# Sublayer boundaries of a two-block transformer kernel: TensorE sums x and the scaled branch in its transposes, token tile 0 is finished first, and GpSimd updates x later

## The chip, the cores and the metric

One Trainium2 chip, one of its cores. The metric is the device time of one execution in microseconds (us); less is better. Three runs of the kernel before stand beside it, and one more execution was taken with the profiler. The engines are named as the profile names them: PE (TensorE, with PEld for its weight loads), DVE (VectorE), ACT (ScalarE), POOL (GpSimd) and SP (SyncE, which here only issues the weight loads).

## What is computed

256 tokens of width 1024 pass two transformer blocks. Cut to what the change touches:

```python
def rms_norm_2(x, g):
    xf = x.astype(jnp.float32)
    y = xf * lax.rsqrt(jnp.mean(xf * xf, axis=-1, keepdims=True) + EPS)
    return (y * g.astype(jnp.float32)).astype(x.dtype)

def swiglu(x, w_gate, w_up, w_down):
    return (jax.nn.silu(x @ w_gate) * (x @ w_up)) @ w_down

for layer in range(DEPTH_2):                      # second block, 2 layers
    if layer == N_A_LAYERS:
        k, v, c = shared_kv(h, kv_norm_g, w_kv, w_fgate, b_fgate)
    f = swiglu(rms_norm_2(h, ffn1_pre_g[layer]), ffn1_w_gate[layer], ffn1_w_up[layer], ffn1_w_down[layer])
    h = h + 0.5 * rms_norm_2(f, ffn1_post_g[layer])
    hn = rms_norm_2(h, mix_pre_g[layer])
    m = recurrent_block(hn, ...) or forgetting_attention(hn, ...)
    h = h + rms_norm_2(m, mix_post_g[layer])
    f = swiglu(rms_norm_2(h, ffn2_pre_g[layer]), ...)
    h = h + 0.5 * rms_norm_2(f, ffn2_post_g[layer])
```

The first block has a mixer, then a mixture of 32 experts (`moe`), each added to x without a norm behind it. All arithmetic is float32.

## The kernel before

**Tiling.** The 256 tokens are two tiles of 128 partitions, t = 0 and t = 1. The residual stream is `x_res` (128 x 2 x 1024). A sublayer reads it transposed, with the channels on the partitions: `xT_hi` and `xT_lo` (8 pieces k of 128 channels, 256 tokens). A float32 product is made of three fast ones (`mm3`, L614): hi x hi, hi x lo, lo x hi, where hi is a value rounded to the fast format and lo is what is missing. Weights stream in pieces of 128 x 1024 through a ring of six slots: SP loads `raw`, ACT writes `w_hi` (`hi`, L1236, or in loops L1301), DVE writes `w_lo = raw - w_hi` (`lo`, L1687, or in loops L1698). The semaphores `hi_done`, `lo_done` and `used` count pieces; ACT may write piece i when piece i - 6 is used.

**Order.** Nothing plans at run time: each engine's program is written out by hand, and the engines meet at counting semaphores. An engine that waits holds back all that stands behind it in its own program.

**A feed-forward** (`feed_forward`, L684, L1303, L1771) takes for each of its 22 (or 32) column blocks f three weight pieces: gate and up (24 products of 256 columns each, into PSUM banks 4 to 7) and down (12 or 24 products of 512 columns, accumulated in banks 0 to 3, two banks for each token tile). DVE multiplies the gate by the row factor `rb` (L1752), ACT applies silu (L1296), and DVE makes the hidden block in `hidden` (times up, times `rb`, for the experts times their weight, then the hi and lo halves, L1758 to L1768). PE runs one block ahead: gate and up of f + 1 come before down of f. The last down writes tile 0, increments `y0_done`, then writes tile 1.

**A boundary between two sublayers** is what the change is about. The program calls them by the number n of the norm that follows: n = 1 (mixer to experts) and n = 2 (experts to the first feed-forward) have a plain residual (`residual`, L1811). n = 3 (feed-forward to recurrent block), 4 (back), 5 (feed-forward to keys and values), 7 (feed-forward to attention), 8 (attention to feed-forward) and the end of the kernel have a norm of the branch y first (`post_norm`, L1821). n = 6 reuses x of n = 5. One with a post norm runs, for each tile t:

1. ACT squares y from PSUM with a row sum and takes the root (`y_squares`, L1333). At n = 3, 5, 7 and the end it starts tile 0 at `y0_done`; at n = 4 and 8 it waits for both tiles.
2. DVE makes the row factor in five tiny steps (`row_rsqrt`, L1714), then `xn = y * factor * gain` (L1828) and `x_res = xn + x_res` (L1831). The gain `g_post` has been broadcast by a DMA from POOL's queue (L581).
3. PE waits for `x_ready`, transposes the eight pieces of the tile into PSUM (L645), and keeps itself at work with dummy products before and between (`keep_warm`, L622; the counts are in the table `WARM`).
4. ACT squares `x_res` for the next norm (`statistics`, L1256), and writes `xT_hi` from the transposes with the gain of the norm (`gained`, L1246); DVE writes `xT_lo` (L1735).
5. PE waits until all four groups of `xT_lo` are there (`xT_ready`), then starts the next sublayer. The row factor of the norm is applied later: DVE makes a diagonal matrix of it (`diag`, L1747), PE spreads it over the partitions with `ones` (`spread`, L651), ACT copies it to `rb` (L1288).

In the code that follows, `channel_major` (L677) is the product of one weight piece with all of xT into one bank.

## Time and profile before

| | us |
|---|---|
| median of 3 runs | 1646.89 |
| lowest, highest | 1646.74, 1649.29 |
| the profiled execution, its own time | 1646.3 |
| its span (first to last instruction) | 1644.5 |
| PE busy in it | 1588.8 (97%) |
| DVE busy | 1062.0 (65%) |
| ACT busy | 784.8 (48%) |
| POOL busy | 43.6 (3%) |
| chain that ended last: share of PE, of DVE | 86%, 8% |

All times of instructions count from the span's start. A product on PE overlaps the next, so a row of `x1` with 0.39 us can be followed by one that starts 0.23 us later; the pace is the distance of the starts. A float32 product that is not split (the dummies, the diagonal spread) is two rows of the trace; a transpose is one. Dummy products count as busy: at a boundary PE's busy share says nothing of useful work. That is why the boundaries are read from the timeline of each engine, from the last product of the old sublayer to the first of the new one.

### The profile page before, as it was taken

To read this page: it belongs to the slowest core of one execution; us is meant where nothing else is said; L and a number is where in the kernel's file an instruction comes from. 1 tells how busy PE (TensorE), PEld (TensorE's weight loads), DVE (VectorE), ACT (ScalarE), POOL (GpSimd) and SP (SyncE) were. 2 spreads that over 40 slices of the span, in tenths; PEclk is the share of its full clock that TensorE was granted. 3 is DMA by queue.
4 is the path that set the end of the run, shared out by engine and by line. 5 is a ranking of instruction groups with operands and counts; after the bars stand their busy time and mean duration, and the time that the engine had idled before them with its cause. 6 is when DMAs were issued, how large, how long until landed. Compare 5 with 4: busy or idle time off the path is not lost.

```text
span 1644.5 us, 27400 instructions
## 1 busy us (share of the span) xinstructions
PE 1588.8 (97%) x10220; PEld 1435.5 (87%) x10220; DVE 1062.0 (65%) x1912; ACT 784.8 (48%) x1151; POOL 43.6 (3%) x68
## 2 busy tenths in 40 slices
PE   8999899999999999999999999999999999999997
PEld 6877778899999899998777999988999989889996
DVE  5358654667666686667585766666766666476665
ACT  6464434444444544435775544455544456454442
POOL 2200000000000300000000000000000000000000
PEclk9999999999999999999999999999999999999999
DMA  8841142755555476664433666645666643356661
GB/s 288 213 154 61 42 145 75 294 184 181 178 189 191 136 215 182 180 190 135 128 97 97 191 181 180 190 128 167 197 187 191 191 130 116 90 167 191 186 183 52
DMA packets 258199, 266.13 MB, mean 162 GB/s; under 512 B 9408, under 2 KB 209392, under 8 KB 257760
## 3 DMA queue, kind: packets, MB, share of 16 engines
q1 hardware_dynamic: 254704, 255.87, 50.7%
q0 software_dynamic: 3440, 9.54, 1.9%
q8 instruction: 33, 0.54, 0.1%
q14 instruction: 22, 0.18, 0.0%
HBM read 264.21 MB, written 1.09 MB: 161 GB/s over the span
## 4 chain that ended last, share of the span: by engine, by line
PE 86%; DVE 8%; ACT 2%; issue 2%; DMA 1%; POOL 0%; DVEq 0%; SPq 0%; ACTq 0%
PE ps L616 27%; PE ps L617 26%; PE ps L618 26%; DVE xT_lo L1735 2%; PE ps L1026 2%; DVE w_lo L1693 1%; DMA arena<-comb_dram 1%; DVE xn L1828 1%; PE ps L626 1%; PE ps L1138 1%; DVE arena L1913 0%; ACT sq L1341 0%; DVE small L1912 0%; PE ps L1148 0%; DVE arena L1938 0%
## 5 line engine op out<-in xcount | busy, mean ns | idle before, releaser
L616 PE MATMUL ps<-xT_hi,w_hi 128*128 128x256 f32 x1696 | 482.9, 285 | 5.9 <-DVE w_lo L1698 3.5
L617 PE MATMUL ps<-xT_lo,w_hi 128*128 128x256 f32 x1696 | 480.6, 283 | 0.0
L618 PE MATMUL ps<-xT_hi,w_lo 128*128 128x256 f32 x1696 | 480.6, 283 | 0.0
L1301 ACT ACTIVATE w_hi<-raw 128x1024 fp32r<-128x1024 f32 x300 | 316.3, 1060 | 246.7 <-PE ps L618 241.9
L1698 DVE TENSOR_TENSOR w_lo<-raw,w_hi 128x1024 fp32r<-128x1024 f32 x300 | 357.4, 1219 | 8.9 <-DMA arena<-comb_dram 8.0
L616 PEld LDWEIGHTS ps<-xT_hi,w_hi 128*128 128x128 f32 x1696 | 325.7, 192 | 12.2 <-DVE xT_lo L1735 4.5
L617 PEld LDWEIGHTS ps<-xT_lo,w_hi 128*128 128x128 f32 x1696 | 325.7, 192 | 3.7
L618 PEld LDWEIGHTS ps<-xT_hi,w_lo 128*128 128x128 f32 x1696 | 325.8, 192 | 0.0
L1693 DVE TENSOR_TENSOR w_lo<-raw,w_hi 128x1024 fp32r<-128x1024 f32 (+4 forms) x185 | 217.8, 1211 | 71.8 <-ACT w_hi L1243 66.8
L1243 ACT ACTIVATE w_hi<-raw 128x1024 fp32r<-128x1024 f32 (+4 forms) x185 | 186.8, 1049 | 70.4 <-PE ps L618 70.4
L616 PE MATMUL ps<-w_hi,hid_hi 128*128 128x512 f32 x480 | 188.5, 393 | 4.4 <-DVE hid_lo L1768 3.1
L1296 ACT ACTIVATE hid_sil<-hid_sil 128x256 f32<-128x256 f32 x120 | 50.5, 421 | 290.0 <-DVE hid_sil L1752 290.0
L617 PE MATMUL ps<-w_lo,hid_hi 128*128 128x512 f32 x480 | 188.0, 392 | 0.0
L618 PE MATMUL ps<-w_hi,hid_lo 128*128 128x512 f32 x480 | 186.8, 389 | 0.0
L1752 DVE TENSOR_TENSOR hid_sil<-ps,rb 128x256 f32<-128x256 f32 x120 | 50.9, 424 | 169.8 <-PE ps L618 154.2
L616 PE MATMUL ps<-w_hi,xT_hi 128*128 128x512 f32 (+3 forms) x392 | 151.8, 387 | 3.8 <-DVE w_lo L1693 2.0
L618 PE MATMUL ps<-w_hi,xT_lo 128*128 128x512 f32 (+3 forms) x392 | 149.7, 382 | 0.0
L617 PE MATMUL ps<-w_lo,xT_hi 128*128 128x512 f32 (+3 forms) x392 | 149.5, 381 | 0.0
L1758 DVE TENSOR_TENSOR hid_sil<-hid_sil,ps 128x256 f32<-128x256 f32 x120 | 50.5, 421 | 147.6 <-PE ps L618 146.5
L616 PEld LDWEIGHTS ps<-w_hi,hid_hi 128*128 128x128 f32 x480 | 90.5, 189 | 21.0 <-DVE hid_lo L1768 3.7
L618 PEld LDWEIGHTS ps<-w_hi,hid_lo 128*128 128x128 f32 x480 | 90.1, 188 | 19.6
L617 PEld LDWEIGHTS ps<-w_lo,hid_hi 128*128 128x128 f32 x480 | 90.5, 189 | 14.6
(338 smaller groups left out, 1991.1 us busy)
## 6 DMA issues: line engine op xcount, KB each, us to landing
raw<-in_ffn_w_gate_dram SPq DMA_DIRECT2D x88, 512.0 KB, 4.1
raw<-in_ffn_w_up_dram SPq DMA_DIRECT2D x88, 512.0 KB, 5.3
raw<-in_ffn_w_down_dram SPq DMA_DIRECT2D x88, 512.0 KB, 4.3
raw<-in_w_in_dram SPq DMA_DIRECT2D x40, 512.0 KB, 5.6
raw<-in_w_gate_dram SPq DMA_DIRECT2D x32, 512.0 KB, 3.6
raw<-in_w_up_dram SPq DMA_DIRECT2D x32, 512.0 KB, 4.0
raw<-in_w_down_dram SPq DMA_DIRECT2D x32, 512.0 KB, 3.6
raw<-in_rg_w_in_dram SPq DMA_DIRECT2D x16, 512.0 KB, 4.8
```

Of the source, the lines that this page charges most:

```text
L616: pe.matmul(o, a_hi, b_hi, start=start, stop=False)
L617: pe.matmul(o, a_hi, b_lo, start=False, stop=False)
L618: return pe.matmul(o, a_lo, b_hi, start=False, stop=stop)
L1026: m = pe.matmul(ps[0:c1 - j * RB, 4 + 2 * z + j // 2, (j % 2) * T:(j % 2 + 1) * T], w[:, g, at:at + c1 - j * RB], cv[:, i, :], start=i == ...
L1243: act.activation(w_hi[0:parts, i % RING, 0:cols], raw[0:parts, i % RING, 0:cols], ACT.Copy)\
L1296: act.activation(sil[:, par, :], sil[:, par, :], ACT.Silu).then_inc(silu_done, 1)
L1301: act.activation(w_hi[:, s, :], raw[:, s, :], ACT.Copy).then_inc(hi_done, 1)
L1693: dve.tensor_tensor(w_lo[0:parts, s, 0:cols], raw[0:parts, s, 0:cols], w_hi[0:parts, s, 0:cols].bitcast(F32), ALU.subtract).then_inc(lo_do ...
L1698: dve.tensor_tensor(w_lo[:, s, :], raw[:, s, :], w_hi[:, s, :].bitcast(F32), ALU.subtract)\
L1735: m = dve.scalar_tensor_tensor(XT[n][1][o], ps[:, 4 + j, k * P:(k + 1) * P], gcol[:, n, 4 * g + k:4 * g + k + 1], XT[n][0][o].bitcast(F32) ...
L1752: dve.tensor_tensor(sil[:, par, :], ps[:, 4 + par, 0:T], rb[:], ALU.mult).then_inc(gate_scaled, 1)
L1758: dve.tensor_tensor(hid[:, par, :], sil[:, par, :], ps[:, 6 + par, 0:T], ALU.mult).then_inc(hid_mul, 1)
```

## The change

For the five boundaries with a post norm and a sublayer behind them:

- DVE makes only `xn = y * gain` (in two halves of 512 columns, `y_gained`), without the row factor. ACT squares each half by itself, in the opposite order, so that both read different banks. The row factor goes into `diag` (`y_diag`).
- PE makes for each of the eight pieces of a tile two float32 products into one PSUM region: x times the identity, and xn times `diag`. The sum is the transposed new x. `x_res` itself is updated later by POOL (`tensor_scalar`, then `tensor_tensor`, 128 x 1024 each), after PE has read the tile.
- The squares of x for the next norm (`statistics`) wait for that update, behind `gained` on ACT.
- The last two down steps of a feed-forward are done for tile 0 first, then for tile 1; likewise the last pieces of the recurrent block's and the attention's output products.
- `first_pair` starts the next sublayer with the products that need only `xT_hi`, half by half, in banks 0 and 1, and makes those with `xT_lo` last. The recurrent block starts with token tile 0 alone (`first_chunk`).
- In `hidden` the product with the up half comes last, behind `rb` and the expert weight, and one `lo` is put between.
- The residuals of n = 1 and 2 are made in halves (`x_part`, `x_ready`). The dummy counts are smaller, the output leaves in four transfers.

```diff
@@ pool (j = 1 to 5)
+                    jn = (3, 4, 5, 7, 8)[j - 1]
+                    for t in range(NT):
+                        pool.wait_ge(y_gained, 4 * (j - 1) + 2 * t + 2)
+                        pool.wait_ge(y_rstd, 2 * (j - 1) + t + 1)
+                        pool.wait_ge(norm_tr, 4 * jn + 2 * t + 2)
+                        pool.tensor_scalar(xn[:, t, :], xn[:, t, :], s_(S_YR + t), None, ALU.mult).then_inc(sig("y_scaled"), 1)
+                        pool.wait_ge(sig("y_scaled"), 2 * (j - 1) + t + 1)
+                        pool.tensor_tensor(x_res[:, t, :], xn[:, t, :], x_res[:, t, :], ALU.add).then_inc(x_ready, 1)
@@ pe
-            WARM = {0: (0, 0, 0), 1: (2, 2, 8), 2: (0, 2, 7), 3: (7, 4, 6), 4: (10, 5, 6), 5: (7, 4, 6), 6: (0, 0, 0),
-                    7: (7, 4, 6), 8: (10, 5, 6)}
+            WARM = {0: (0, 0, 12), 1: (2, 2, 8), 2: (0, 0, 3), 3: (2, 0, 0), 4: (2, 0, 2), 5: (2, 0, 2), 6: (0, 0, 0),
+                    7: (2, 0, 2), 8: (2, 0, 2)}
+                    pe.wait_ge(y_gained, 4 * j + 2 * t + 2)
+                    pe.wait_ge(y_diag, 2 * j + t + 1)
...
+                            o = ps[:, 4 + 2 * t + g, k * P:(k + 1) * P]
+                            pe.matmul(o, v[:, 4 * g + k, :], ident, start=True, stop=False)
+                            m = pe.matmul(o, z[:, 4 * g + k, :], diag[:, t, :], start=False, stop=True)
+            def first_pair(n, i, outs, steps):
+                for z in range(2):
+                    pe.wait_ge(lo_done, i + z + 1)
...
+                for g in range(2):
+                    pe.wait_ge(norm_hi, 4 * n + 3 + g)
+                    for z, (hi, lo) in enumerate(views):
+                        for k in range(4 * g, 4 * g + 4):
+                            pe.matmul(outs[z], hi[:, k, :], xT_hi[:, k, :], start=k == 0, stop=False)
+                            pe.matmul(outs[z], lo[:, k, :], xT_hi[:, k, :], start=False, stop=False)
+                pe.wait_ge(xT_ready, 4 * (n + 1))
+                for z, (hi, lo) in enumerate(views):
+                    for k in range(KT):
+                        m = pe.matmul(outs[z], hi[:, k, :], xT_lo[:, k, :], start=False, stop=k == KT - 1)
+                    m.then_inc(used, steps[z])
@@ pe, end of feed_forward
+                down(c0 + n - 1, b + 3 * n - 1, 0, False, False, tiles=(0,))
+                down(c0 + n, b + 3 * n, 1, False, True, s=s, tiles=(0,))
+                down(c0 + n - 1, b + 3 * n - 1, 0, False, False, tiles=(1,))
+                down(c0 + n, b + 3 * n, 1, False, True, s=s, tiles=(1,))
@@ dve, post_norm
-                    link(dve.scalar_tensor_tensor(z, ps[:, 2 * t:2 * t + 2, :], s_(S_YR + t),
-                                                  g_post[:].rearrange("p (a c) -> p a c", a=2), ALU.mult, ALU.mult))
-                    dve.tensor_tensor(xv, xn[:, t, :], xv, ALU.add).then_inc(x_ready, 1)
+                    for h in (1, 0):
+                        if h == 0:
+                            dve.wait_ge(y_ssq, 4 * j + 2 * t + 1)
+                        dve.tensor_tensor(xn[:, t, h * WID:(h + 1) * WID], ps[:, 2 * t + h, :], g_post[:, h * WID:(h + 1) * WID],
+                                          ALU.mult).then_inc(y_gained, 1)
...
+                    if j < 5:
+                        dve.tensor_scalar(diag[:, t, :], ident, s_(S_YR + t), None, ALU.mult).then_inc(y_diag, 1)
+                        continue
```

PE at n = 4, behind the last product of the recurrent block (`con` holds the identity and the dummies' operand), before:

```order
1812 L626 MATMUL ps<-con 128x256 x10
1813 L645 MATMUL ps<-con,x_res 128x128 x8
1814 L626 MATMUL ps<-con 128x256 x5
1815 L645 MATMUL ps<-con,x_res 128x128 x8
1816 L626 MATMUL ps<-con 128x256 x6
1817 L616 MATMUL ps<-xT_hi,w_hi 128x256
```

The same place now, the first pieces of tile 0, then the first of tile 1 and the start of the feed-forward (with the waits):

```order
2125 L642 MATMUL ps<-con 128x256 x2
2126 L662 MATMUL ps<-con,x_res 128x128 [waits y_diag,y_gained]
2127 L663 MATMUL ps<-diag,xn 128x128
...
2142 L662 MATMUL ps<-con,x_res 128x128 [waits y_diag,y_gained]
2143 L663 MATMUL ps<-diag,xn 128x128
...
2158 L642 MATMUL ps<-con 128x256 x2
2159 L729 MATMUL ps<-xT_hi,w_hi 128x256 [waits norm_hi,lo_done]
2160 L730 MATMUL ps<-xT_hi,w_lo 128x256
```

The 8 transposes of a tile became 16 float32 products, the dummies went from 21 calls to 4, and the feed-forward starts with products that read `xT_hi` alone.

ACT at the same boundary before, from the squares of y to the first square of x:

```order
401 L1341 ACTIVATE sq,small<-ps 128x1024 [waits used]
402 L1344 ACTIVATE small<-small,con 128x1 [waits y_ssq]
403 L1341 ACTIVATE sq,small<-ps 128x1024 [waits used]
404 L1344 ACTIVATE small<-small,con 128x1 [waits y_ssq]
405 L1259 ACTIVATE sq,small<-x_res 128x1024 [waits x_ready]
406 L1261 ACTIVATE small<-small,con 128x1 [waits norm_ssq]
407 L1252 ACTIVATE xT_hi<-ps,gcol 128x128 [waits norm_tr]
```

And now, from the last group of `xT_hi` to the weight pieces of the feed-forward:

```order
419 L1328 ACTIVATE xT_hi<-ps,gcol 128x128 [waits norm_tr]
420 L1328 ACTIVATE xT_hi<-ps,gcol 128x128 x3
421 L1335 ACTIVATE sq,small<-x_res 128x1024 [waits x_ready]
422 L1337 ACTIVATE small<-small,con 128x1 [waits norm_ssq]
423 L1335 ACTIVATE sq,small<-x_res 128x1024 [waits x_ready]
424 L1337 ACTIVATE small<-small,con 128x1 [waits norm_ssq]
425 L1319 ACTIVATE w_hi<-raw 128x1024 [waits used,raw_in2]
```

Both squares of x stand behind `xT_hi` now, and their `x_ready` comes from POOL; the weight pieces stand behind them.

POOL's program at n = 4 had only the `g_post` transfer. It now has, ahead of it:

```order
57 L593 TENSOR_SCALAR xn<-xn,small 128x1024 [waits norm_tr,y_rstd,y_gained]
58 L595 TENSOR_TENSOR x_res<-xn,x_res 128x1024 [waits y_scaled]
59 L593 TENSOR_SCALAR xn<-xn,small 128x1024 [waits norm_tr,y_rstd,y_gained]
60 L595 TENSOR_TENSOR x_res<-xn,x_res 128x1024 [waits y_scaled]
61 L597 DMA g_post<-in_ffn_post_g_dram 128x1024 [waits post_used]
```

Two pairs of elementwise operations came to POOL's queue at each of the five boundaries.

## Rows read from the trace of the kernel before

**Rows 1.** The page: the granted PE clock in 40 slices, in tenths of full speed

```profile
PEclk9999999999999999999999999999999999999999
```

**Rows 2.** Timeline of PE at n = 3: start us, us, line, operation, [idle before]

```profile
744.72 0.40 PE L616 MATMUL ps<-w_hi,hid_hi 128*128 128x512 f32 x1
...
749.96 0.39 PE L618 MATMUL ps<-w_hi,hid_lo 128*128 128x512 f32 x1
750.19 3.18 PE L626 MATMUL ps<-con 128*128 128x256 f32 x14
...
761.53 0.50 PE L616 MATMUL ps<-w_hi,xT_hi 128*128 128x512 f32 x1 [0.40 <-DVE xT_lo L1735]
```

**Rows 3.** Timeline of PE at n = 4, to the spread of the row factor

```profile
894.52 4.48 PE L626 MATMUL ps<-con 128*128 128x256 f32 x20
...
907.21 0.38 PE L616 MATMUL ps<-xT_hi,w_hi 128*128 128x256 f32 x1 [0.39 <-DVE xT_lo L1735]
...
915.94 0.60 PE L655 MATMUL ps<-diag,con 128*128 128x128 f32 x4
```

**Rows 4.** Timeline of ACT at n = 3

```profile
742.50 0.42 ACT L1296 ACTIVATE hid_sil<-hid_sil 128x256 f32<-128x256 f32 x1 [7.13 <-DVE hid_sil L1752]
742.83 1.99 ACT L1243 ACTIVATE w_hi<-raw 128x1024 fp32r<-128x1024 f32 x2
...
749.03 1.03 ACT L1341 ACTIVATE sq<-ps 128x1024 f32<-128x1024 f32 x1 [2.69 <-PE ps L618]
749.95 0.19 ACT L1341 ACTIVATION_READ_ACCUMULATOR sq<-ps 128x1 f32 x1
750.18 0.30 ACT L1344 ACTIVATE small<-small,con 128x1 f32<-128x1 f32 x1
...
755.32 2.16 ACT L1252 ACTIVATE xT_hi<-ps,gcol 128x128 fp32r<-128x128 f32 x8
```

**Rows 5.** Timeline of DVE at n = 3

```profile
744.99 0.42 DVE L1758 TENSOR_TENSOR hid_sil<-hid_sil,ps 128x256 f32<-128x256 f32 x1 [2.52 <-PE ps L618]
...
746.24 0.42 DVE L1768 TENSOR_TENSOR hid_lo<-hid_sil,hid_hi 128x256 fp32r<-128x256 f32 x1
...
750.58 0.16 DVE L1720 RECIPROCAL small<-small 128x1 f32<-128x1 f32 x1 [0.17 <-ACT small L1344]
...
751.36 1.28 DVE L1828 SCALAR_TENSOR_TENSOR xn<-ps,small,g_post 128x1024 f32<-128x1024 f32 x1
752.68 1.23 DVE L1831 TENSOR_TENSOR x_res<-xn,x_res 128x1024 f32<-128x1024 f32 x1
```

**Rows 6.** Timeline of DVE at n = 4: diagonals of the norm, then weight pieces

```profile
909.20 0.29 DVE L1747 TENSOR_SCALAR diag<-con,small 128x128 f32<-128x128 f32 x1
909.40 2.35 DVE L1693 TENSOR_TENSOR w_lo<-raw,w_hi 128x1024 fp32r<-128x1024 f32 x2
```

**Rows 7.** Timeline of PE at n = 2: last down, transposes of both tiles, the feed-forward

```profile
553.92 0.39 PE L618 MATMUL ps<-w_hi,hid_lo 128*128 128x512 f32 x1
554.55 1.16 PE L645 MATMUL ps<-con,x_res 128*128 128x128 f32 x8 [0.23 <-DVE x_res L1819]
...
556.41 1.04 PE L645 MATMUL ps<-con,x_res 128*128 128x128 f32 x8
...
561.35 0.39 PE L616 MATMUL ps<-xT_hi,w_hi 128*128 128x256 f32 x1 [0.88 <-DVE xT_lo L1735]
```

**Rows 8.** Timeline of PE at n = 5: dummies, then the first product of the keys

```profile
1096.04 3.18 PE L626 MATMUL ps<-con 128*128 128x256 f32 x14
...
1107.37 0.39 PE L616 MATMUL ps<-xT_hi,w_hi 128*128 128x256 f32 x1 [0.39 <-DVE xT_lo L1735]
```

**Rows 9.** Groups of instructions on POOL: the one that computes on columns

```profile
L595 POOL MEMSET arena<- 112x5376 f32 x1 | 4.6, 4578 | 268.5 <-DVE x_res L1819 268.5
```

**Rows 10.** Groups by line: weight loads of the transposes (x count | us, mean ns)

```profile
L645 PEld LDWEIGHTS ps<-con,x_res 128*128 128x128 f32 x144 | 18.9, 197 | 15.7 <-DVE x_res L1831 8.9 <-issue 5.1 <-DVE x_res L1819 1.5
```

**Rows 11.** Timeline of DVE at n = 2: both residuals

```profile
553.27 2.35 DVE L1819 TENSOR_TENSOR x_res<-ps,x_res 128x1024 f32<-128x1024 f32 x2
```

**Rows 12.** Timeline of DVE at the end of the kernel: the last update of x

```profile
1640.24 1.22 DVE L1831 TENSOR_TENSOR x_res<-xn,x_res 128x1024 f32<-128x1024 f32 x1
```

More of the change, by code:

```diff
@@ L651, in spread, with norm @@
+            def norm(n):
+                for t in range(NT):
+                    norm_tile(n, t)
+                keep_warm(WARM[n][2], 3)
             def spread(n, bank):
@@ L695, in up, with down @@
                     channel_major((s + 1) % RING, ps[:, 6 + par, 0:T], PLAN.step(b + 1) if f == 0 else 1, xT)
-                def down(hc, i, par, first, last):
-                    s = (b + 3 * (1 - par) + 2) % RING
+                def down(hc, i, par, first, last, s=None, tiles=range(NT)):
+                    if s is None:
+                        s = (b + 3 * (1 - par) + 2) % RING
                     pe.wait_ge(hid_ready, hc)
                     pe.wait_ge(lo_done, i + 1)
-                    for t in range(NT):
+                    for t in tiles:
                         c = slice(t * P, (t + 1) * P)
@@ L707, in down @@
                                     w_hi[:, s, r], w_lo[:, s, r], first, last)
-                    m.then_inc(used, 1)
-                up(0, b, 0)
+                    m.then_inc(used if 1 in tiles else sig("half_down") if not last else y0_done, 1)
+                if norm_n is None:
+                    up(0, b, 0)
+                else:
+                    first_pair(norm_n, b, (ps[:, 0, 0:T], ps[:, 1, 0:T]), (1, PLAN.step(b + 1)))
                 if after_first:
@@ L1054, in rg_in, with first_chunk @@
                                 k0 == 0, k0 + kn == KT)
-            rg_in(0, 4)
+            def first_chunk(t, pieces):
+                for q in pieces:
+                    i = PLAN.start["rgin"] + q
+                    pe.wait_ge(lo_done, i + 1)
+                    hi, lo = slot_view(w_hi, i % RING, 2, WID), slot_view(w_lo, i % RING, 2, WID)
+                    for k in range(2):
+                        m = mm3(ps[:, t, :], xT_hi[:, 2 * q + k, t * P:(t + 1) * P], xT_lo[:, 2 * q + k, t * P:(t + 1) * P],
+                                hi[:, k, :], lo[:, k, :], q == 0 and k == 0, q == 3 and k == 1)
+                    if t:
+                        m.then_inc(used, 1)
+            norm_tile(3, 0)
+            norm_tile(3, 1)
+            for q in range(4):
+                pe.wait_ge(xT_ready, 4 * 3 + 1 + q // 2)
+                first_chunk(0, (q,))
+            pe.wait_ge(xT_ready, 4 * 3 + 4)
+            first_chunk(1, range(4))
+            rg_in(4, 4)
             rec_transposes(0)
@@ L1186, in o_half @@
                     m.then_inc(used, 1)
-            q_half(0, 0)
-            q_half(0, 1)
+                elif k == KT - 1:
+                    m.then_inc(y0_done, 1)
+            first_pair(7, PLAN.start["q"], (ps[:, 0, 0:T], ps[:, 1, 0:T]), (1, 1))
             spread(7, 5)
-            for j in (1, 2):
-                for half in range(2):
-                    q_half(j, half)
+            for half in range(2):
+                q_half(2, half)
+            q_half(3, 0)
             pe.wait_ge(sig("fk_rows"), 32)
@@ L1741, in norm @@
                         lo(2 * t + 1)
+                if beside:
+                    beside()
                 if n != 6:
@@ L1783, in step @@
                     c = c0 + f + 1
-                    hidden(c, b + 3 * f + 2, f % 2, f if moe else None, c, f + 1)
+                    hidden(c, b + 3 * f + 2, f % 2, f if moe else None, c, f + 1, banks[1], beside)
                 if pre:
```

256 lines of the change are left out of this document (150 added, 106 removed).

## The prediction

> **What bounds the kernel now.** I read the page's busy shares first (the table above): PE is busy 97% of the span, at the upper of its two clocks, 2.4 GHz, in all 40 slices [rows 1]. The chain that ended last is PE for 86%. But dummies count as busy, so the next view is the timeline of each engine at the boundaries. Call E the moment at which PE could issue the next product behind the old sublayer's last. At n = 3, E = 750.19 and the first useful product starts at 761.53: 11.34 us, filled with 13 + 4 calls of dummies and 16 transposes [rows 2]. n = 5 has the same (1096.04 to 1107.37 [rows 8]); n = 7 runs the same program, I take the same. At n = 4, where ACT waits for both tiles, it is 907.21 - 894.52 = 12.69 us [rows 3]; n = 8 runs the same program, I take the same. In these windows PE waits for a chain ACT, DVE, PE, ACT, DVE [rows 4, 5], tile after tile. Everywhere else the products of PE follow each other at their pace, so the kernel changes by what the boundaries change. There are five with a post norm, n = 2 (experts to feed-forward), n = 1 and the end.
>
> **Tile 0 earlier.** The last two downs now give tile 0 first: 12 products of 512 columns at (749.96 - 744.72) / 23 = 0.228 us [rows 2] are 2.73 us of head start instead of 1.37. The price is that the hidden block is wanted one half down earlier. PE reaches the second down of tile 0 at 744.72 + 1.37 = 746.09. The hidden block's last three steps, now behind the up product (0.42 + 0.29 + 0.42 with gaps, 1.2 us from 744.99), end at 746.2, and the `lo` that was put between must wait for ACT, whose first of two weight pieces ends at 743.8 [rows 4, 5]; it ends at 745.05. So PE waits 0.25 us at n = 3, 5, 7 and the end. At n = 2 the expert weight stands behind that `lo` too: 0.65 us.
>
> **Until tile 0's diagonal is there.** ACT's square costs 1.03 us for 1024 columns and 0.42 for 256 [rows 4], so 0.62 for 512, with the row sum's read 0.75. Two of them 1.5 (DVE's gained halves, some 0.7 each, run beside them on the other bank), the added small activation and the root 0.3 each: 2.1. DVE's four small steps at 0.2 and a diagonal of 0.29 [rows 5, 6]: 3.2 us behind tile 0's end, which is E - 2.57. That is E + 0.6. PE has two dummy calls (4 rows of 3.18 / 14 = 0.227 us [rows 2]) until E + 0.9. So PE is not late for tile 0, and tile 1's diagonal comes at E + 3.8, while PE is at tile 0.
>
> **The products that replace the transposes.** 16 float32 products of 128 columns a tile, two rows each. A dummy row of 256 columns takes 0.227 us, half of it is 0.114; the transposes of 128 columns, each with its own weights, have starts (1.04 - 0.27) / 7 = 0.11 us apart in the second tile [rows 7], and the diagonal spread has the same pace of 0.11 [rows 3]. I take 32 x 0.114 = 3.63 us a tile, 7.3 for both, and 0.12 for the first start behind an idle moment, as the first tile of transposes shows (1.16 against 1.04). Before it was 1.0 a tile. This is the largest addition: 5.3 us a boundary, but it stands in place of waiting. PE ends tile 1 at E + 8.3 and, with two dummy calls at n = 4, 5, 7, 8, reaches the next sublayer at E + 9.2. There `first_pair` needs only three groups of `xT_hi` (ACT takes 1.1 us a group [rows 4] and follows PE group by group); the last group is there at E + 9.5, the last of `xT_lo` at E + 10.6, and they are wanted at E + 11.1 and E + 13. Nothing is waited for. Gross gain: 12.69 - 9.2 = 3.5 us at n = 4 and 8; 11.34 - 9.2 - 0.25 = 1.9 at n = 5 and 7; 11.34 - 8.3 - 0.25 = 2.8 at n = 3.
>
> **What is late next.** On ACT the squares of x now stand behind `xT_hi` and wait for POOL's update, and the weight pieces of the new sublayer stand behind them. POOL can start tile 1 when PE is done with it, E + 8.3. Call P the time of POOL's pair (scale, then add) for a tile. Then the square with read (1.16), the root (0.3) and the first weight piece on ACT (1.0) [rows 4] end at E + 10.8 + P; DVE's `lo` for it (1.2 [rows 6]) ends at E + 12 + P. DVE itself is ready by then: its four small steps and the diagonal run beside that piece and end 0.15 later than it, so E + 12.2 + P. PE wants this piece behind `first_pair`, whose 48 products take 2 x 2.9 us (three pieces from 907.21 to 915.94 [rows 3]): at E + 9.2 + 5.8 = E + 15. The stall is P - 2.8.
>
> No row shows an elementwise operation on POOL. The nearest are its memset, 4.58 us for 5376 columns, 0.85 ns a column [rows 9], and DVE's own pair of the same size, 1.28 + 1.23 = 2.5 us [rows 5]. If reads and writes overlapped fully, P would be 2 x 0.87 = 1.75; if each of the five streams (two for the scale, three for the add) took the memset's rate, 4.35. I take the middle between DVE's 2.5 and 4.35 and its hand-over of 0.1, P = 3.5, and keep 1.75 and 5.0 (twice DVE) as ends. The stall is then 0.7 to 0.8 at n = 4, 8 and 5; at n = 7 PE has the spread to do first, 0.5. At n = 3 the next pieces are ACT's and DVE's work before the squares, but behind all of `xT`: the third is ready at E + 8.3 + 1.1 + 1.1 + 1.2 = 11.8 and wanted two quarter steps of 1.37 behind E + 8.3: 0.8 us.
>
> The Trainium skill speaks against this move: GPSIMD Engine Reference, section 3 (Performance versus the Vector engine), gives 4497 ns for an add of 2048 columns against 2293 on VectorE, and advises VectorE for elementwise work. DVE's 1.23 us here for 1024 agrees with its half; no row shows POOL's half. By its figure the add would be about 2.25 us and P, with the scale near the one-input rate, 3.3 to 3.5.
>
> **n = 2, n = 1, the end.** At n = 2 DVE's two `lo` before the residual (they held it until 553.27 [rows 11]) are one now, tile 0 is done earlier, and PE need not wait for `xT_lo`. ACT becomes the bound: from PE's transposes of tile 0 at E + 1.1 four groups of 1.06 us; `first_pair` starts at its third, E + 4.6 with the 0.65 of the hidden block, against 561.35 - (553.92 + 0.23) = 7.2 before [rows 7]: 2.5 us gained. At n = 1 two half residuals cost 0.15 us more than one whole before the first square, which stays ahead there: -0.15. At the end tile 1's update was over at 1641.46 [rows 12]; by the steps above, with one tile of DVE work in front, it comes at 1640.5: 0.95 gained.
>
> **Sum.** n = 3: 2.8 - 0.8 = 2.0. n = 4 and 8: 3.5 - 0.75 = 2.75 each, 5.5. n = 5: 1.9 - 0.7 = 1.2. n = 7: 1.9 - 0.5 = 1.4. n = 2: 2.5. n = 1: -0.15. End: 0.95. Together 13.4 us. The loops lose nothing: the two forms of `hidden` have equal work on DVE, and PE wants the result 8 us later. What PE waits for before the first down stays, since the same chain follows the spread. The profiled execution took 1646.3, 1.8 more than its span and 0.6 below the median of 1646.89; I carry the difference over: 1646.9 - 13.4 = 1633.5 us.
>
> **Rivals.**
>
> *GpSimd at half of VectorE's speed in both operations.* P = 5.0: 1.5 us more at four boundaries, 6 together: 1639.5. For: the memset is no faster a column than DVE is. Against: the scale has one input. The skill's advice above would have it so. Chance 15%.
>
> *GpSimd so slow that the kernel gets slower.* Each us of P beyond 3.5 costs four. The whole gain is eaten at P = 3.5 + 13.4 / 4 = 6.85 us, 3.4 an operation, which is 2.7 times DVE. At P = 7.6 the time is 1633.5 + 4 x 4.1 = 1649.9. At n = 7 the rows of `fq` behind POOL's pair would come late as well. Chance 6%.
>
> *The weight loads show.* A load takes 197 ns in the records [rows 10] against the pace of 0.11. If float32 products with fresh weights in both rows could not hide it, a tile would take 32 x 0.197 = 6.3 us, 2.7 more, ten times: 27 us, 1660.5. Against: the transposes load fresh weights with the same strides at the pace of 0.11 to 0.126 [rows 7]. At 0.126 it is 0.4 a tile, 4 us: 1637.5, in my range. Chance of the full case 4%.
>
> *The clock falls.* PE has fewer dummies. If the gaps let the granted clock fall to 1.2 GHz at five boundaries and each then ran 3 us of work at half speed, it would be 15 us: 1648.5. Against: PE stands idle under 1 us in a row in my timeline. Chance 3%.
>
> *It does not do what it says.* ACT and DVE hand halves to each other, and if tile 0's diagonal came 2.5 us later than E + 0.6, tile 0 would gain nothing by being first and each of the five would lose 2.2: 1644.5, within 0.2%. Chance 3%.
>
> **Numbers.** Forecast 69%; its own ends are P = 1.75 (no stalls, 2.7 us less: 1630.8) and the slower pace with P a little up (1638). With the 15% of half speed the range is 1630 to 1641, which leaves out the last four. Faster by over 0.2% (3.3 us, about what a measurement of this kernel can tell from none): 86%. Within: 4%. Slower: 10%.
>
> **What would show it.** PE's 64 rows of float32 products a boundary in 7.3 us; the first useful product at E + 8.3 (n = 3) and E + 9.2; PE's idle time behind DVE's `w_lo` of 0.5 to 0.8 at n = 4, 5, 7, 8; POOL's two operations summing to 3.5 us. Wrong, if POOL's pair exceeds 5 us, if a tile takes over 4.1 us, or if PE waits for `y_diag`.

## The result, and the profile of the changed kernel

The changed kernel is slower, where the prediction had it faster.

| | before | after |
|---|---|---|
| median of 4 runs each, us | 1648.09 | 1684.87 |
| lowest to highest, us | 1646.74 to 1649.65 | 1682.66 to 1686.06 |
| ratio after/before, 95% interval | | 1.0221 (1.0204 to 1.0239) |
| span of the profiled execution, us | 1644.5 | 1682.0 |

The forecast was 1633.5 us, with a range of 1630 to 1641. The span grew by 37.5 us where the sum had it 13.4 shorter: 50.9 us have to be found.

The page of the changed kernel, busy times and the chain that ended last (answers to [rows 1]):

```profile
PE 1624.2 (97%) x10298; PEld 1476.0 (88%) x10298; DVE 1058.8 (63%) x1942; ACT 793.2 (47%) x1187; POOL 96.9 (6%) x88
...
PE 87%; DVE 6%; ACT 3%; POOL 1%; DMA 1%; issue 1%; DVEq 0%; SPq 0%; ACTq 0%; POOLq 0%
PE ps L632 25%; PE ps L633 25%; PE ps L634 25%; PE ps L662 2%; PE ps L663 2%; DVE w_lo L1778 2%; PE ps L1081 2%; PE ps L642 1%; DMA arena<-comb_dram 1%; POOL xn L593 1%; PE ps L1213 1%; POOL x_res L595 1%; ACT w_hi L1319 0%; DVE xT_lo L1820 0%; DVE arena L2027 0%
```

PE's share is the 97% of before, so the busy shares alone show nothing of the loss. The chain names the new lines: 662 and 663, the products that replace the transposes, with 2% each, and POOL's two operations with 1% each. The timeline of PE at n = 3, to be read beside [rows 2], shows the first of them:

```profile
748.59 1.02 PE L642 MATMUL ps<-con 128*128 128x256 f32 x4
749.53 0.71 PE L662 MATMUL ps<-con,x_res 128*128 128x128 f32 x2
750.08 0.64 PE L663 MATMUL ps<-diag,xn 128*128 128x128 f32 x2
750.56 0.64 PE L662 MATMUL ps<-con,x_res 128*128 128x128 f32 x2
...
764.36 0.64 PE L663 MATMUL ps<-diag,xn 128*128 128x128 f32 x2
...
768.62 0.47 PE L632 MATMUL ps<-w_hi,xT_hi 128*128 128x512 f32 x1 [0.88 <-DVE w_lo L1778]
```

A call (two rows) follows the other after 0.475 us, 0.238 a row. The last one listed starts 0.475 us before PE is free again at 764.8, so the 32 calls take 15.2 us. The prediction had 0.114 a row and 7.3 us. That is 7.9 us at each of five boundaries, 39.7 us in all. Beside it stands the weight load, in the groups of the weight loads by form (answers to [rows 10]; the last two numbers are busy us and mean ns of one):

```profile
L663 PEld LDWEIGHTS ps<-diag,xn 128*128 128x128 f32 x160 | 45.9, 335 | 0.0
L662 PEld LDWEIGHTS ps<-con,x_res 128*128 128x128 f32 x160 | 45.7, 334 | 1.2 <-issue 1.2
L677 PEld LDWEIGHTS ps<-con,x_res 128*128 128x128 f32 x64 | 9.4, 201 | 5.9 <-issue 5.2 <-DVE x_res L1911 0.3
L690 PEld LDWEIGHTS ps<-diag,con 128*128 128x128 f32 x24 | 3.2, 190 | 3.7 <-DVE diag L1834 3.7
```

The loads of the new products take 0.335 us. The transposes that are left (line 677) load `x_res` through the same view in 0.201, and the spread, whose columns are neighbours, in 0.190.

The second part is POOL. Its groups, and then its timeline at n = 4:

```profile
L593 POOL TENSOR_SCALAR xn<-xn,small 128x1024 f32<-128x1024 f32 x10 | 28.5, 2845 | 810.7 <-PE ps L663 810.7
L595 POOL TENSOR_TENSOR x_res<-xn,x_res 128x1024 f32<-128x1024 f32 x10 | 24.8, 2478 | 0.8
```

```profile
907.40 2.84 POOL L593 TENSOR_SCALAR xn<-xn,small 128x1024 f32<-128x1024 f32 x1 [134.94 <-PE ps L663]
910.32 2.36 POOL L595 TENSOR_TENSOR x_res<-xn,x_res 128x1024 f32<-128x1024 f32 x1
915.00 2.85 POOL L593 TENSOR_SCALAR xn<-xn,small 128x1024 f32<-128x1024 f32 x1 [2.32 <-PE ps L663]
917.94 2.40 POOL L595 TENSOR_TENSOR x_res<-xn,x_res 128x1024 f32<-128x1024 f32 x1
```

The pair P is 5.3 us, not 3.5, and the operation with one input is the slower one. Who waits for it is PE at n = 4:

```profile
914.64 1.03 PE L642 MATMUL ps<-con 128*128 128x256 f32 x4
...
919.33 2.08 PE L734 MATMUL ps<-xT_lo,w_hi 128*128 128x256 f32 x16
...
924.21 0.39 PE L632 MATMUL ps<-xT_hi,w_hi 128*128 128x256 f32 x1 [2.80 <-DVE w_lo L1778]
```

PE is done with the first pair of weight pieces and waits 2.80 us for the next `w_lo`. VectorE makes it from ScalarE's piece, and that piece stands behind ScalarE's square of the x that POOL ended at 920.34:

```profile
920.37 1.06 ACT L1335 ACTIVATE sq<-x_res 128x1024 f32<-128x1024 f32 x1 [3.01 <-POOL x_res L595]
...
921.75 2.94 ACT L1319 ACTIVATE w_hi<-raw 128x1024 fp32r<-128x1024 f32 x3
```

The third part is the clock. It follows in the windows of the same place (length, PE busy and rows, granted clock, DMA share, GB/s):

```profile
915.00:922.00 7.00, 6.41 (x52) 1.00 0.03 12
922.00:925.00 3.00, 0.79 (x6) 1.00 0.49 172
925.00:928.00 3.00, 3.00 (x16) 0.50 0.74 206
928.00:935.00 7.00, 5.96 (x41) 0.97 0.48 139
```

Behind the stall the granted clock is 0.50 of full speed, 1.2 instead of 2.4 GHz, for about 3.3 us: half of it, 1.7 us, is lost. The same stands at n = 7 (0.50 from 1393 to 1396); at n = 8, with the same stall of 2.80 us, the clock stays up.

Taken together: products 39.7; stalls of PE behind POOL 0.9 + 2.8 + 2.3 + 2.1 + 2.8 = 10.9 (n = 3, 4, 5, 7, 8) where 3.5 had been forecast, 7.4 more; half clock at two places, 3.3. That is 50.4 us against the 50.9 to be found. At n = 5 and 7 the stall is two waits, 1.66 us for the diagonal behind POOL and 0.62 and 0.42 for the next `w_lo`. This is a reading of two traces; the experiments had to show that the parts are causes.

### The profile page after: what moved, and what is told of

The parts are those of the page before. It is cut to its first block, busy times and chain, and to the rows that moved or that the text cites. A ratio compares the mean times of both kernels' runs of the same rounds, so it can differ in the third digit from the quotient of the medians.

```text
span 1682.0 us, 27655 instructions
## 1 busy us (share of the span) xinstructions
PE 1624.2 (97%) x10298; PEld 1476.0 (88%) x10298; DVE 1058.8 (63%) x1942; ACT 793.2 (47%) x1187; POOL 96.9 (6%) x88
## 4 chain that ended last, share of the span: by engine, by line
PE 87%; DVE 6%; ACT 3%; POOL 1%; DMA 1%; issue 1%; DVEq 0%; SPq 0%; ACTq 0%; POOLq 0%
PE ps L632 25%; PE ps L633 25%; PE ps L634 25%; PE ps L662 2%; PE ps L663 2%; DVE w_lo L1778 2%; PE ps L1081 2%; PE ps L642 1%; DMA arena<-comb_dram 1%; POOL xn L593 1%; PE ps L1213 1%; POOL x_res L595 1%; ACT w_hi L1319 0%; DVE xT_lo L1820 0%; DVE arena L2027 0%
## 5 line engine op out<-in xcount | busy, mean ns | idle before, releaser
L632 PE MATMUL ps<-xT_hi,w_hi 128*128 128x256 f32 x1616 | 461.6, 286 | 9.8 <-DVE w_lo L1778 6.6
L633 PE MATMUL ps<-xT_lo,w_hi 128*128 128x256 f32 x1616 | 459.3, 284 | 0.0
L634 PE MATMUL ps<-xT_hi,w_lo 128*128 128x256 f32 x1616 | 459.2, 284 | 0.0
L632 PEld LDWEIGHTS ps<-xT_hi,w_hi 128*128 128x128 f32 x1616 | 311.7, 193 | 15.1 <-DVE w_lo L1778 7.6
L633 PEld LDWEIGHTS ps<-xT_lo,w_hi 128*128 128x128 f32 x1616 | 312.0, 193 | 3.6
L634 PEld LDWEIGHTS ps<-xT_hi,w_lo 128*128 128x128 f32 x1616 | 311.9, 193 | 0.0
L1839 DVE TENSOR_TENSOR hid_sil<-ps,rb 128x256 f32<-128x256 f32 x120 | 50.9, 424 | 226.4 <-PE ps L634 215.9
```

Source lines behind the costliest of these rows:

```text
L632: pe.matmul(o, a_hi, b_hi, start=start, stop=False)
L633: pe.matmul(o, a_hi, b_lo, start=False, stop=False)
L634: return pe.matmul(o, a_lo, b_hi, start=False, stop=stop)
L1839: dve.tensor_tensor(sil[:, par, :], ps[:, bank, 0:T], rb[:], ALU.mult).then_inc(gate_scaled, 1)
```

## Experiments

All of them were run beside the kernel before, whose medians were 1647.9 to 1648.2 us and whose single runs lay between 1645.5 and 1651.5. So a single run (e1, e3, e6) can be 3 us off.

### Which reads are slow: e1_steps

```
-                    v = x_res[:, t, :].rearrange("p (c k) -> p k c", k=KT)
-                    z = xn[:, t, :].rearrange("p (c k) -> p k c", k=KT)
+                    step = {3: 8, 4: 1, 5: 2, 7: 4, 8: 8}[n]
...
+                            if n == 8:
+                                pe.matmul(o, ident, part(x_res, 4 * g + k), start=True, stop=False)
+                                m = pe.matmul(o, diag[:, t, :], part(xn, 4 * g + k), start=False, stop=True)
```

> The changed kernel with one thing varied by boundary: how far apart in memory the 128 values lie that one weight load of the replacement products reads on each partition. Norm 3: every 8th float (as changed), norm 4: neighbours, norm 5: every 2nd, norm 7: every 4th. At norm 8 the operands are swapped: identity and row factor are the stationary ones (neighbouring columns), and x and the scaled branch with their step of 8 are the moving ones. From norm 4 on the values are therefore not those of the reference (channels are taken in another order, at norm 8 nothing is transposed); the work is the same in kind and count. Theory S (the step of the stationary read is what the products pay): a call of the 160 takes 0.475 us at norm 3 (0.238 a row, 2 rows), 0.22 to 0.25 at norm 4 (0.11 to 0.12 a row), and also about 0.23 at norm 8; the weight loads of norm 4 take about 0.19 us against 0.336 at norm 3; norms 5 and 7 show where it sets in. Theory F (a float32 product that is no transpose pays 0.238 a row whatever it reads): 0.475 us a call at all five. Theory M (what is slow is a strided read of either operand by such a product): norm 8 stays at 0.475, norm 4 falls.

Measured: 1674.48 us in one run. The records of line 670 (x) in windows around n = 3, 4, 5 and 7, and of line 667 (operands swapped) at n = 8; numbers are min/median/max ns, then the starts of the first and the last:

```profile
L670 PEld LDWEIGHTS ps<-con,x_res x32: 312/335/336, 753.8 to 768.3; 128*128 128x128 f32 x32
L670 PEld LDWEIGHTS ps<-con,x_res x32: 189/192/192, 903.6 to 910.5; 128*128 128x128 f32 x32
L670 PEld LDWEIGHTS ps<-con,x_res x32: 194/196/197, 1108.0 to 1115.2; 128*128 128x128 f32 x32
L670 PEld LDWEIGHTS ps<-con,x_res x32: 308/329/332, 1360.2 to 1374.4; 128*128 128x128 f32 x32
L667 PEld LDWEIGHTS ps<-x_res,con x32: 186/208/208, 1456.1 to 1470.2; 128*128 128x128 f32 x32
```

The boundaries do the same 32 calls each, and a line holds half of their rows. With a step of 8 or 4 floats they spread over 14.5 and 14.2 us, with a step of 1 or 2 over 6.9 and 7.2. The last line is the surprise: identity and row factor are loaded in 0.208 us, and the calls still spread over 14.1 us, since now the moving operand has the step of 8. Theory F (the operation) falls at n = 4 and 5, theory S (only the stationary read) falls at n = 8, theory M stands: a float32 product takes twice the time when its stationary operand is read with a step of 4 or 8 floats, or its moving one with a step of 8 (other steps of the moving operand were not run).

The Trainium skill has a rule for this which the prediction did not weigh: SBUF — State Buffer, section "Door 1: The DMA port swizzle", speaks of lines of 16 bytes that want at least two accesses each for full speed. With two accesses a line a step of 2 floats is free and one of 4 is not, and this is where the trace has its edge (a load of 0.196 us against one of 0.329). The same passage gives 4 float32 as how far one can stride for free; here a step of 4 is not free, and the measurement decides.

### Is it the products alone: e2_contig and e3_contig_add

e2 reads neighbours at all five boundaries, so the channels come out in another order; e3 does so too and leaves POOL's scaling out, which makes P 2.4 us:

```
-                    v = x_res[:, t, :].rearrange("p (c k) -> p k c", k=KT)
-                    z = xn[:, t, :].rearrange("p (c k) -> p k c", k=KT)
+                    v = x_res[:, t, :].rearrange("p (k c) -> p k c", k=KT)
+                    z = xn[:, t, :].rearrange("p (k c) -> p k c", k=KT)
```

```
-                        pool.tensor_scalar(xn[:, t, :], xn[:, t, :], s_(S_YR + t), None, ALU.mult).then_inc(sig("y_scaled"), 1)
-                        pool.wait_ge(sig("y_scaled"), 2 * (j - 1) + t + 1)
```

> The changed kernel with the stationary operands of the replacement products read as neighbouring floats at all five boundaries; the channels therefore come out in another order than the reference's, the number and size of all operations is the same. Theory S: 32 calls a boundary fall from 15.2 to 7.3 us, which is 5 x 7.9 = 39.7 us, less what GpSimd's update then keeps waiting. With its pair at 5.3 us (measured in the changed kernel) the next product stalls by 5.3 - 2.8 = 2.5 us at the five boundaries where the prediction had 0.7, but part of this stall stands in the changed kernel already, and at norms where the longer products hid it, it comes up: 1684.9 - 39.7 = 1645, and up to 5 x 2.5 more hidden or not: 1640 to 1652. Theory F: 1685, within 2.

> As e2_contig, and GpSimd's scaling of the branch before its addition is left out, so that x takes the unscaled branch (the values are not the reference's): GpSimd's work a tile falls from 5.3 to about 2.4 us. If GpSimd's update is on the path (the first product that needs the second tile's channel sums, or the products behind the first pair, wait 2.5 us or more for VectorE's conversions, which follow it), this is shorter than e2_contig by 2 to 3 us at each of up to five boundaries, 5 to 15 us. If it is off the path: the same within 1 us.

Measured: e2 1654.74 us (1653.91 to 1659.17), ratio to before 1.0049 (1.0032 to 1.0065); e3 1633.93 us in one run. So the step of the read is worth 30.1 us here and not 39.7, and GpSimd's scaling is worth 20.8, more than the 5 to 15 expected. The waits of PE in e2 (us in total, times, longest; 2.3 of the 12.8 stand at the kernel's start and not at a boundary):

```profile
PE ps L632 <- DVE w_lo L1778: 12.8, 4, 4.5
PE ps L690 <- DVE diag L1834: 6.7, 2, 3.4
```

and its timelines at n = 4, of POOL and of PE:

```profile
895.85 2.84 POOL L593 TENSOR_SCALAR xn<-xn,small 128x1024 f32<-128x1024 f32 x1 [131.03 <-PE ps L663]
898.78 2.38 POOL L595 TENSOR_TENSOR x_res<-xn,x_res 128x1024 f32<-128x1024 f32 x1
901.13 2.84 POOL L593 TENSOR_SCALAR xn<-xn,small 128x1024 f32<-128x1024 f32 x1
904.06 2.38 POOL L595 TENSOR_TENSOR x_res<-xn,x_res 128x1024 f32<-128x1024 f32 x1
```

```profile
898.83 0.39 PE L663 MATMUL ps<-diag,xn 128*128 128x128 f32 x2
899.05 1.03 PE L642 MATMUL ps<-con 128*128 128x256 f32 x4
...
910.31 0.39 PE L632 MATMUL ps<-xT_hi,w_hi 128*128 128x256 f32 x1 [4.48 <-DVE w_lo L1778]
```

PE has done tile 1 at 899.05, but POOL is busy with tile 0 until 901.16 and starts tile 1 only then. The prediction let POOL begin with tile 1 when PE is done with it (stall = P - 2.8 = 2.5). With the 2.1 us of queue it is 4.6; the trace has 4.48. As soon as P exceeds what PE needs for a tile (3.6 us), each further us of P counts twice. In e3 the queue is gone (POOL in the timeline at n = 4):

```profile
900.37 2.36 POOL L593 TENSOR_TENSOR x_res<-xn,x_res 128x1024 f32<-128x1024 f32 x1 [135.70 <-PE ps L661]
903.93 2.40 POOL L593 TENSOR_TENSOR x_res<-xn,x_res 128x1024 f32<-128x1024 f32 x1 [1.20 <-PE ps L661]
```

and PE's waits behind POOL at n = 4, 5, 7 and 8 with it. The time is then 1633.9, but that this is almost the prediction's 1633.5 is luck. The start of the first down with a fresh hidden block behind n = 2, up to which e2 and e3 are the same program, is 4.8 us later in e3's one run:

```profile
572.48 0.50 PE L632 MATMUL ps<-w_hi,hid_hi 128*128 128x512 f32 x1 [1.04 <-DVE hid_lo L1857]
```

```profile
577.32 0.50 PE L630 MATMUL ps<-w_hi,hid_hi 128*128 128x512 f32 x1 [1.04 <-DVE hid_lo L1855]
```

From there to the end of the span e3 takes 1054.7 us and the kernel before 1069.9 (from 574.60). That is 15.2 us less, where the prediction's terms for this part, without the stalls that hang on P, add up to 3.5 x 2 + 1.9 x 2 + 2.8 - 0.8 + 0.95 = 13.8. So with fast products and a short P the rest of the sum held.

### The half clock behind a stall: e9_contig_warm

The stalls at the five boundaries are 16.2 us longer in e2 than in e3; the times differ by 20.8, and the traces from the first down behind n = 2 on by 25.7. e9 is e2 with dummies in the four long waits:

```
                     first_pair(norm_n, b, (ps[:, 0, 0:T], ps[:, 1, 0:T]), (1, PLAN.step(b + 1)))
+                    if norm_n in (4, 8):
+                        keep_warm(9, 3)
...
+            keep_warm(7, 3)
             spread(5, 7)
...
+            keep_warm(7, 3)
             spread(7, 5)
```

> As e2_contig, with dummy products in the four places where PE stood idle for 3.3 to 4.5 us behind GpSimd's pairs (9 calls, 4.1 us, behind the first pair at n = 4 and 8; 7 calls, 3.2 us, ahead of the spread at n = 5 and 7). In e2 the granted clock is 0.50 for 3.4 to 6.8 us behind each of these stalls. If that half speed is what makes e2 and e3 differ by 20.9 us, while the stalls themselves are only 16.2, this kernel is 4 to 8 us faster than e2: 1647 to 1651, and its clock shows 1.00 there. If the clock costs nothing there: 1654.7, within 1.

Measured: 1648.66 us (1646.38 to 1652.62), ratio to before 1.0003 (0.9991 to 1.0015), 6.1 us below e2. Windows at n = 4, first of e2, then of e9:

```profile
911.00:915.00 4.00, 4.00 (x25) 0.61 0.76 219
```

```profile
911.00:915.00 4.00, 3.42 (x17) 1.00 0.40 147
```

The chain behind POOL is as long as before (from the end of tile 1 to the next weight piece's product 11.3 us in both), only its consequence is gone: the half clock behind POOL's stalls cost e2 6 us. What is left of the 25.7 beside stalls and these 6, some 3.5 us, is not explained.

### Do the two causes add: e10_strided_add

The changed kernel with its step of 8, but without POOL's scaling (the diff of e3's second part alone).

> The changed kernel, products read with their step of 8 as in the change, but GpSimd's scaling left out (x takes the unscaled branch, so the values are not the reference's). It completes the square with the changed kernel (1684.9), e2_contig (1654.7) and e3_contig_add (1633.9). The slow products end a tile 3.95 us later than the fast ones, so GpSimd's first pair has room before the second begins, and less of it shows: the stalls of the changed kernel behind GpSimd (2.8 at n = 4 and 8, 1.7 at n = 5 and 7) should vanish, and the half clock behind them: 9 to 14 us less, 1671 to 1676. If the two causes are independent, it is the full 20.8 less, 1664; then the products would cost 30 in both rows. My theory says they are not, since PE's products and GpSimd's pairs stand beside each other.

Measured: 1671.81 us (1669.56 to 1672.93), ratio 1.0144 (1.0126 to 1.0163).

PE's waits behind POOL at n = 4, 5, 7 and 8 are gone from its trace. The table has the times and, in brackets, the part from the first down behind n = 2 to the end of the span, which leaves out the scatter of the part that no edit touches:

| us | scale and add, P = 5.3 | add alone, P = 2.4 | difference |
|---|---|---|---|
| step 8 | 1684.9 (1109.3) | 1671.8 (1094.8) | 13.1 (14.5) |
| neighbours | 1654.7 (1080.4) | 1633.9 (1054.7) | 20.8 (25.7) |
| difference | 30.1 (28.9) | 37.9 (40.1) | |

Without POOL in the way the step of the read costs 37.9 us by the times and 40.1 by the traces, where the count of calls gives 39.7. With POOL in the way 8 to 11 us of it are hidden: the slow products keep POOL's pairs apart, and PE's stalls behind POOL are 10.9 us in the changed kernel against 17.2 in e2. The two costs stand beside each other and don't add.

### Why the transposes did not show it: e6_transposes

```
-                            pe.matmul(o, v[:, 4 * g + k, :], ident, start=True, stop=False)
-                            m = pe.matmul(o, z[:, 4 * g + k, :], diag[:, t, :], start=False, stop=True)
+                            pe.transpose(o, v[:, 4 * g + k, :], ident)
+                            m = pe.transpose(o, z[:, 4 * g + k, :], ident)
```

> The changed kernel, where each replacement product is a TensorE transpose of the same strided columns (x, then the scaled branch over it in the same bank, unscaled): reads with the same step of 8, same count of calls, but no float32 product; the values are not the reference's, since nothing is added. After e1 a product that reads either operand with a step of 4 or 8 floats takes 0.467 to 0.475 us, with a step of 1 or 2 0.227 to 0.233. Theory P (the step is dear only for a float32 product): the transposes take 0.11 to 0.125 us each with loads of 0.19 to 0.2, so 32 take 3.6 us a boundary, 11.6 less than in the changed kernel; the time is 1684.9 minus up to 58 plus what GpSimd's queued pairs (5.3 us a tile) then keep waiting, 1640 to 1660. Theory Q (two loads of strided columns in a row are dear in any operation, and the transposes of before only hid it by being few): 0.2 us or more a call.

Measured: 1645.47 us in one run. PE at n = 5, and the group of the loads:

```profile
1099.74 0.28 PE L663 MATMUL ps<-con,xn 128*128 128x128 f32 x1
1099.86 0.28 PE L662 MATMUL ps<-con,x_res 128*128 128x128 f32 x1
```

```profile
L662 PEld LDWEIGHTS ps<-con,x_res 128*128 128x128 f32 x80 | 15.6, 196 | 11.4 <-issue 11.4
```

32 transposes a boundary with the step of 8 keep 0.11 us each, with loads of 0.196. So theory P stands, and with it the flaw of my argument: the transposes of before did say 0.11 a call at this step, but what holds for them doesn't hold for a product. (At n = 3 of this kernel they are 0.213 apart; there PE had waited for the diagonal and the granted clock was 0.59.) Why a transpose is spared is not shown by any run, and the Trainium skill's rule on lines, in the section cited above, does not make that difference.

### What the change is worth without both: e4, e5, e7

e4_dve_update keeps tile 0 first and the early first pair, and takes back the rest: post norm and update of x on VectorE ahead of the transposes, with dummy counts of its own and the output in two transfers. Core of its diff to the changed kernel:

```
-        POST = {3: 0, 4: 1, 5: 2, 7: 3, 8: 4}
+        POST = {}
...
-                        pool.tensor_scalar(xn[:, t, :], xn[:, t, :], s_(S_YR + t), None, ALU.mult).then_inc(sig("y_scaled"), 1)
...
-                        pool.tensor_tensor(x_res[:, t, :], xn[:, t, :], x_res[:, t, :], ALU.add).then_inc(x_ready, 1)
...
+                    link(dve.scalar_tensor_tensor(z, ps[:, 2 * t:2 * t + 2, :], s_(S_YR + t),
+                                                  g_post[:].rearrange("p (a c) -> p a c", a=2), ALU.mult, ALU.mult))
+                    xv = x_res[:, t, :]
+                    dve.tensor_tensor(xv, xn[:, t, :], xv, ALU.add).then_inc(x_ready, 1)
```

> Only a part of the change: token tile 0 is finished first and the first pair of channel-major products may start on the first half of the channels, but the post norm and x's update are on VectorE as before, x is updated ahead of the norm, and the norm transposes x as before; the replacement products and GpSimd's update are gone. If the replacement products and GpSimd carry the whole loss, this keeps what the earlier tile 0 gives: 1.9 to 2.5 us at norm 2, about 1 at the end, and at each boundary some 3.4 us (norms 3, 5, 7) to 5 us (4, 8): 1624 to 1632, faster than the kernel before by 1.0 to 1.5%. If the order of the tiles itself costs (split squares, more semaphore steps), it is at or above 1648.

Measured: 1627.11 us (1624.55 to 1629.43), ratio 0.9871 (0.9852 to 0.9891): faster than both kernels. PE at n = 3:

```profile
752.94 1.89 PE L632 MATMUL ps<-con 128*128 128x256 f32 x8
755.35 1.16 PE L667 MATMUL ps<-con,x_res 128*128 128x128 f32 x8 [0.52 <-DVE x_res L1910]
756.34 2.32 PE L632 MATMUL ps<-con 128*128 128x256 f32 x10
758.77 1.16 PE L667 MATMUL ps<-con,x_res 128*128 128x128 f32 x8
759.96 0.50 PE L622 MATMUL ps<-w_hi,xT_hi 128*128 128x512 f32 x1
```

From E = 752.94 to the next useful product it is 7.0 us: before 11.34 [rows 2], forecast for the change 8.3, in the change 16.2 (748.59 to 764.8). The transposes behind VectorE's update are ahead even of the 8.3 that fast products would have given, because 32 products at their best pace take 7.3 us of PE and 16 transposes 2.

e5_dve_no_pair is e4 with the first pair back in its old form:

```
-                pe.wait_ge(xT_ready, 4 * (n + 1))
...
+                pe.wait_ge(xT_ready, 4 * (n + 1))
+                for z in range(2):
+                    pe.wait_ge(lo_done, i + z + 1)
+                    channel_major((i + z) % RING, outs[z], steps[z])
```

> As e4_dve_update, but the first pair of channel-major products again waits for all of the new channels (hi and lo) and runs in the order of before. What remains of the change is token tile 0 first. The first pair wants three of four groups of xT_hi, where the full start waits for one more group of hi (1.1 us on ScalarE) and its lo (1.1 us on VectorE): if it pays, this kernel is slower than e4 by 1 to 2 us at n = 2, 4, 5, 7 and 8, 5 to 10 us, near 1635. If it doesn't (the stall behind it takes it back), within 1 us of e4's 1627.1. Either way it should stay below the 1648 of before by what tile 0's head start gives (some 1.4 us at eight places).

Measured: 1641.91 us (1636.95 to 1645.93), ratio 0.9964 (0.9953 to 0.9976), 14.8 us slower than e4, more than the 5 to 10 expected. PE at n = 4:

```profile
899.90 0.58 PE L622 MATMUL ps<-xT_hi,w_hi 128*128 128x256 f32 x1 [2.54 <-DVE xT_lo L1795]
900.71 0.41 PE L622 MATMUL ps<-xT_hi,w_hi 128*128 128x256 f32 x1
```

It waits 2.54 us for the last of `xT_lo`, and three products then take 0.64 us instead of 0.36, the half clock again. The kernel before filled this wait with dummies, e5 doesn't, so part of the 14.8 is the clock's. (The spans of the profiled executions, 1635.2 and 1625.1, are only 10.1 apart, but e4's is 4.3 us behind at n = 1 already, 293.56 against 289.25, where the two still do the same.) So the first pair carries most of the 21 us that e4 gains over before. The other 6.0 stand for all that is left, the order of the tiles above all, and were not separated.

e7_halves_dve takes the halves of the change (squares beside gained branch) and one VectorE operation for the update:

```
-                        dve.tensor_scalar(diag[:, t, :], ident, s_(S_YR + t), None, ALU.mult).then_inc(y_diag, 1)
+                        dve.scalar_tensor_tensor(x_res[:, t, :], xn[:, t, :], s_(S_YR + t), x_res[:, t, :], ALU.mult, ALU.add)\
+                            .then_inc(x_ready, 1)
                         continue
```

> The halves of the change (squares and gained branch by halves beside each other on ScalarE and VectorE, tile 0 first, the first pair) with the update of x on VectorE in one operation from the gained branch (scale and add, 1.28 us), and the transposes of before; no GpSimd, no replacement products. Against e4_dve_update the chain of a tile loses one VectorE operation of 1.23 us and gains two half operations of some 0.7 that run beside the squares: about 0.7 us less a boundary, five times 3.5: 1623.6. If VectorE, which now does both tiles' halves and updates in one queue, is the bound there, no gain: 1627.

Measured: 1628.47 us (1624.37 to 1630.02), ratio 0.9871 (0.9854 to 0.9888): no gain over e4. At n = 3 its x is ready for tile 1 at 758.24, where e4 has 758.72, but counted from E (752.32 and 752.94) that is 5.9 us against 5.8. VectorE does both tiles' halves, small steps and updates in one queue, and PE still waits 1.25 us for it.

## Why the prediction was wrong, step by step

- **What bounds the kernel.** Right: the time moved only at the boundaries.
- **Tile 0 earlier** and **until tile 0's diagonal is there.** Right: PE did not wait for `y_diag` at n = 3 in the changed kernel, and the hidden block of n = 2 held it 0.49 us (forecast 0.65). At n = 3, 5 and 7 and at the end the hidden block held nothing (forecast 0.25). e4 shows what these steps are worth without the rest.
- **The products that replace the transposes.** This step failed. Its term of 0.114 us a row measured 0.238; 7.3 us a boundary became 15.2, 39.7 us in all. It was taken from a dummy, from transposes and from the spread: the first and the last read neighbours [rows 2, 3], and the transposes [rows 7] read with the step but are no products. None of the three had both. e1 and e6 show that it takes both. The rival "the weight loads show" had the right place with 4% and the wrong size: it took the load of 0.197 [rows 10] as the worst, 27 us, and the load itself grew to 0.335. It was argued away with the transposes' pace, which e6 shows to be true and beside the point.
- **What is late next.** P was mis-sized: 5.3 instead of 3.5, outside the 1.75 to 5.0 kept as ends. Nine of the ten adds took 2.36 to 2.40 us. The estimate from the figure of the Trainium skill (GPSIMD Engine Reference, section 3) was about 2.25, and the trace nearly agrees. The scale was 2.85, and there section 4.1 of the same page of the Trainium skill, which calls operations with one input roughly line-rate, differs from the trace: it is the slower of the two. And stall = P - 2.8 lacked the queue: it held where PE's slow products kept the tiles apart (2.80 measured, 2.5 by the formula, in the changed kernel), and missed 2.1 us in e2. The break-even of the second rival (P = 6.85, "each us of P beyond 3.5 costs four") was wrong for the same reason: e2 is slower than before (1.0049) at P = 5.3.
- **The clock falls.** Given 3% as a case of its own with 15 us. It came, but as a follower of POOL's stalls: two places of 1.7 us in the changed kernel, 6 us in e2 (e9). The argument against it, that PE stands idle under 1 us in my timeline, hung on the stalls being small.
- **n = 2, n = 1, the end.** Near. The first down with a fresh hidden block behind n = 2 starts at 572.67, before at 574.60: 1.9 us for n = 1 and 2 together, forecast 2.35. Of this n = 1 is a loss of 0.24 (303.57 against 303.33, forecast 0.15). At the end tile 1's update is over 6.4 us behind the start of PE's last product, before 7.4: 0.9 gained, forecast 0.95.
- **The numbers.** 10% for slower, as a sum of rivals of which two, the loads and GpSimd, came true together. They share no cause, but each was priced against a kernel in which the other was well. Two of the signs that the prediction named for being wrong came: POOL's pair over 5 us (5.3), and a tile over 4.1 us (7.6).

## What to carry to other kernels

A float32 product whose operand is a strided view is priced from a product with such a view, not from a transpose or a product of neighbours; if no row has it, both ends of the range come from the load, and a step of 4 or 8 floats is a reason to expect twice the time a call. When work is moved to an engine that serves two tiles in turn, each us of its time counts once as long as it is shorter than the gap between the tiles, and twice beyond. And where PE is kept busy only to hold its clock, each new stall carries a second price behind it, which a dummy in its place takes away.

## What the runs showed of the hardware that was not expected

- A float32 product of 128 columns takes 0.233 to 0.238 us a row instead of 0.11 to 0.12 when its stationary operand is read with a step of 4 or 8 floats, or its moving one with a step of 8 (e1); with a step of 2 of the stationary one it doesn't. The weight load shows it (0.329 to 0.336 against 0.192 to 0.196 us) only if the stationary operand is the strided one. A transpose with the same step keeps 0.11.
- GpSimd scales 1024 columns a partition by a row factor in 2.85 us and adds two tensors of that size in 2.4 (changed kernel).
- VectorE's small operations can be held while GpSimd computes. In the changed kernel at n = 4 the last of the small steps, one column, took 2.31 us, the one in front of it 0.16:

```profile
917.85 0.16 DVE L1807 SCALAR_TENSOR_TENSOR small<-small 128x1 f32<-128x1 f32 x1
918.04 2.31 DVE L1808 SCALAR_TENSOR_TENSOR small<-small 128x1 f32<-128x1 f32 x1
```

It begins 0.10 us behind POOL's add (917.94) and ends with it (920.34). The Trainium skill (GPSIMD Engine Reference, section 8) says that GpSimd shares its SBUF interfaces with VectorE and contends with VectorE's instructions that have two SBUF inputs; this one has two, and the trace agrees. It is no single case: at n = 5, 7 and 8 the same step took 2.30 to 2.31 us beside POOL's second add, and at n = 3 another one with two tensor inputs (line 1806) took 1.98 and ended with the add. The steps with one input that began inside an add, at n = 3, kept their 0.15 and 0.16, and so did all small steps beside POOL's scaling. It goes the other way too: POOL's add at n = 3 began while VectorE was still at a `w_lo`, and took 3.39 us instead of 2.40. No run isolated it, so the cause is not shown.
